# One product of keys and queries for both directions of a gated scan

## What is computed

```python
def _gla_scan(q, k, log_f, v, s0):
    mask = tril(ones(64, 64))
    def step(S, inp):                                   # chunks of 64 tokens
        qc, kc, gc, vc = inp
        b = cumsum(gc, axis=2)
        decay = exp(where(mask, b[:, :, :, None] - b[:, :, None], -inf))
        scores = einsum("bhtk,bhsk,bhtsk->bhts", qc, kc, decay)
        o = einsum("bhts,bhsv->bhtv", scores, vc) + einsum("bhtk,bhkv->bhtv", qc * exp(b), S)
        S = exp(b_end)[..., None] * S + einsum("bhsk,bhsv->bhkv", kc * exp(b_end - b), vc)
        return S, o

o_f, s_f = _gla_scan(qh, kf, gf, vh, s0_f)
o_b, s_b = _gla_scan(flip(qh), flip(kb), flip(gb), flip(vh), s0_b)
o = o_f + flip(o_b)
```

## Time and profile before

| | |
|---|---|
| median of 3 runs | 3245.99 us (3244.85 to 3246.26) |
| the profiled execution | 3246.3 us |
| its span, first to last instruction | 3244.5 us |
| TensorE busy | 2983.4 us, 92% |
| VectorE, ScalarE, GpSimd busy | 854.6, 561.9, 99.8 us |
| mean granted TensorE clock | 0.955 |
| slabs of L969, chain's share | 38% |
| scores (L1054), busy | 95.1 us in 768 instructions |

### The profile page before, as it was taken

How to read it: one execution, slowest core, us unless ns; L and a number is a source line. 1 busy time by engine, 2 the same in 40 slices (tenths; PEclk the granted TensorE clock), 3 DMA queues, 4 the chain that set the end, 5 groups by cost and what they waited for, 6 DMA issues and landing times.

```text
span 3244.5 us, 37753 instructions
## 1 busy us (share of the span) xinstructions
PE 2983.4 (92%) x16694; PEld 2469.0 (76%) x16694; DVE 854.6 (26%) x1777; ACT 561.9 (17%) x814; POOL 99.8 (3%) x204
## 2 busy tenths in 40 slices
PE   6999999999999999999999999799989998676665
PEld 4878889988888788878888888688878887343332
DVE  1201045531554210010014553410046313111111
ACT  1100232113221110010033115210012331100000
POOL 0000001100110000000001010000000000000000
PEclk8999999999999999999999999899989999788888
DMA  8566433344333566654443334244433235699997
GB/s 317 222 255 252 149 137 128 117 145 153 130 120 126 200 223 240 224 221 153 151 151 135 121 134 144 81 152 155 149 114 127 104 104 233 291 431 429 430 430 334
DMA packets 74311, 641.79 MB, mean 198 GB/s; under 512 B 8096, under 2 KB 13344, under 8 KB 22432
## 3 DMA queue, kind: packets, MB, share of 16 engines
q1 hardware_dynamic: 68720, 631.27, 51.7%
q10 hardware_dynamic: 5424, 8.05, 0.7%
HBM read 638.24 MB, written 1.05 MB: 197 GB/s over the span
## 4 chain that ended last, share of the span: by engine, by line
PE 82%; DMA 12%; DVE 3%; ACT 2%; issue 1%; ACTq 0%; POOL 0%; DVEq 0%
PE ps L969 38%; PE ps L992 17%; DMA work<-in_w_moe 10%; PE ps L1154 6%; PE ps L1054 3%; PE ps L1003 3%; PE ps L980 2%; PE ps L1180 2%; PE ps L949 2%; PE ps L846 2%; PE ps L865 1%; DVE work L1578 1%; DMA ones<-in_ones 1%; DMA ring<-in_w_moe 1%; PE ps L1161 1%
## 5 line engine op out<-in xcount | busy, mean ns | idle before, releaser
L969 PE MATMUL ps<-h,ring 128*128 128x256 f32 x6016 | 1323.4, 381 | 6.2 <-ACT h L1338 6.2
L969 PEld LDWEIGHTS ps<-h,ring 128*128 128x128 f32 x6016 | 1140.1, 191 | 173.7 <-issue 18.9
L992 PE MATMUL ps<-work,ring 128*128 128x256 f32 x2464 | 542.4, 380 | 0.0
L992 PEld LDWEIGHTS ps<-work,ring 128*128 128x128 f32 x2464 | 464.5, 190 | 69.0 <-issue 6.6
L1578 DVE TENSOR_TENSOR work<-work,ps 128x512 f32<-128x512 f32 (+1 forms) x153 | 87.9, 574 | 773.0 <-PE ps L969 713.6
L1154 PE MATMUL ps<-h,ring 128*128 128x256 f32 x928 | 207.9, 383 | 6.6 <-DVE h L1584 6.6
L1154 PEld LDWEIGHTS ps<-h,ring 128*128 128x128 f32 x928 | 176.9, 192 | 34.9 <-issue 11.5
L1578 DVE TENSOR_TENSOR work<-work 128x128 f32<-128x128 f32 (+4 forms) x632 | 195.7, 367 | 29.5 <-ACT work L1357 13.9
L846 PE MATMUL ps<-work 128*32 128x256 f32 x1536 | 120.5, 483 | 81.5 <-DMA work<-in_w_moe 75.7
L846 PEld LDWEIGHTS ps<-work 128*32 128x32 f32 x1536 | 67.2, 138 | 133.4 <-issue 121.3
L1305 ACT ACTIVATE work<-ps 128x512 f32<-128x512 f32 x77 | 46.0, 597 | 649.5 <-PE ps L969 649.3
(11 more groups left out here) (250 smaller groups left out, 1899.4 us busy)
## 6 DMA issues: line engine op xcount, KB each, us to landing
ring<-in_w SPq DMA_DIRECT2D x182, 1024.0 KB, 4.8
work<-in_w_moe SPq DMA_DIRECT2D x32, 4096.0 KB, 23.4
ring<-in_w_in SPq DMA_DIRECT2D x80, 1024.0 KB, 4.7
ring<-in_w_ada SPq DMA_DIRECT2D x72, 1024.0 KB, 6.1
ring<-in_w_moe SPq DMA_DIRECT2D x16, 4096.0 KB, 24.5
ring<-in_w SPq DMA_DIRECT2D x56, 896.0 KB, 4.6
ring<-in_w_out SPq DMA_DIRECT2D x16, 1024.0 KB, 4.8
ring<-in_w_mem SPq DMA_DIRECT2D x4, 1024.0 KB, 4.8
```

The costliest lines, as they stand in the source:

```text
L969: last = nc.tensor.matmul(ps[:, b, c * L:c * L + L], w[:, k * L + c * P:k * L + c * P + P], h[:, k, cols], start=(k == 0), stop=(k == KD - 1))
L992: last = nc.tensor.matmul(ps[:, b, c * L:c * L + L], w[:, k * L + c * P:k * L + c * P + P], hid[:, k0 + k, :], start=(k0 + k == 0 and c == 0),
```

## The change

The array `ex[:, 0, lev]` of a level now holds keys of both directions, and `ex[:, 1, lev]` queries of both: at each level the forward direction's key blocks are the backward direction's query blocks, so each array is full. One product then gives both directions' scores of a tile; its mask keeps both off-diagonal quarters. The eighth product uses `ksum`, the sum of both directions' keys, formed once a pass into the half of `glamask` that is free now. Score and value stages go by head and tile. The plan gives a head six bundles, one of them empty; the decays of a head follow the last products of the head before. In the first pass (28 gaps) there are 27 bundles and not 28, in the second (30) 27 and not 28, in the third (30) 25 and not 26. The semaphores' counts are halved where stages are. The core of the diff:

```diff
 def heads(l, s):
-    for hd in range(8):
-        more = hd + 1 < 8
-        out.append([("score", l, s, hd, 0)] + ([("decay", l, s, hd + 1)] if more else []))
-        out.append([("score", l, s, hd, 1), ("value", l, s, hd, 0)] + ([("times", l, s, hd + 1)] if more else []))
-        out.append([("value", l, s, hd, 1)] + ([("inter", l, s, hd)] if l == 0 else [])
-                   + ([("head", l, s, hd // 2)] if hd % 2 else []))
+    out = [[("decay", l, s, 1)], [("times", l, s, 0)]]
+    for hh in range(4):
+        out += [[], [("score", l, s, hh, 0)], [("score", l, s, hh, 1), ("value", l, s, hh, 0)]]
+        last = [("value", l, s, hh, 1)] + ([("inter", l, s, hh)] if l == 0 else []) + [("head", l, s, hh)]
+        if hh + 1 < 4:
+            out += [last + [("decay", l, s, 2 * hh + 2)], [("decay", l, s, 2 * hh + 3)], [("times", l, s, hh + 1)]]
+        else:
+            out.append(last)
     return out
...
-    side = [[("gmlp", 0, 1), ("decay", 0, 1, 0)], [("times", 0, 1, 0)]] + heads(0, 1) + [[("osquare", 0, 1)], [("osum", 0, 1)]]
+    side = [[("gmlp", 0, 1), ("decay", 0, 1, 0)]] + heads(0, 1) + [[("osquare", 0, 1)], [("osum", 0, 1)]]
...
-        gm = shaped(glamask[:], 2, 8, P)
+        gm = shaped(glamask[:, 0:8 * P], 8, P)
+        ksum = shaped(glamask[:, 8 * P:16 * P], 4, L)
...
                         for lev in range(8):
-                            lo, hi = (ex[:, d, lev, tc],) * 2 if lev < 7 else (kk[:, d, hh, tc], qq[:, hh, tc])
+                            kl, ql = (ex[:, 0, lev, tc], ex[:, 1, lev, tc]) if lev < 7 else (ksum[:, hh, tc], qq[:, hh, tc])
...
-                    elif kind == "decay":
+                    elif kind == "decay" and stage[3] % 2:
                         l, s, hd = stage[1:]
-                        act.wait_ge(dec_in, 8 * PASS[l, s] + hd + 1)
-                        nc.scalar.activation(ex[:, hd % 2, :, :], ex[:, hd % 2, :, :], ACT.Exp)
-                        nc.scalar.activation(eb[:, s, hd, :], be[:, s, hd, :], ACT.Exp).then_inc(dec_out, 1)
+                        act.wait_ge(dec_in, 4 * PASS[l, s] + hd // 2 + 1)
+                        nc.scalar.activation(ex[:, 0, :, :], ex[:, 0, :, :], ACT.Exp).then_inc(dec_out, 1)
+                        nc.scalar.activation(ex[:, 1, :, :], ex[:, 1, :, :], ACT.Exp)
+                        nc.scalar.activation(eb[:, s, hd - 1:hd + 1, :], be[:, s, hd - 1:hd + 1, :], ACT.Exp).then_inc(dec_out, 1)
...
+                def both_keys(l, s):
+
+                    if PASS[l, s]:
+                        dve.wait_ge(sc_done, 8 * PASS[l, s])
+                    else:
+                        dve.wait_ge(const_in, 16 * N_CONST)
+                    own(tt(ksum, kk[:, 0], kk[:, 1], add))
...
                         l, s, hd = stage[1:]
-                        d = hd % 2
-                        if hd >= 2 and l == 0:
-                            dve.wait_ge(hd_done, 8 * PASS[l, s] + hd - 1)
-                        elif hd >= 2:
-                            dve.wait_ge(pv_done, 32 + 2 * (hd - 1))
+                        hh, d = divmod(hd, 2)
+                        p = PASS[l, s]
+                        if hh and d == 0:
+                            dve.wait_ge(sc_done, 8 * p + 2 * hh)
+                            if l == 0:
+                                dve.wait_ge(hd_done, 4 * p + hh)
                         early, late, ee, le = sums(hd, s)
                         for lev in range(6):
...
-                            dst_e, dst_l = early_late(blocks(ex[:, d, lev, :], m), d)
+                            keys, _ = early_late(blocks(ex[:, 0, lev, :], m), d)
+                            _, queries = early_late(blocks(ex[:, 1, lev, :], m), d)
...
-                        dve.wait_ge(dec_out, 8 * PASS[l, s] + hd + 1)
-                        for lev in range(7):
-                            m = 1 << lev
-                            _, late = early_late(blocks(ex[:, d, lev, :], m), d)
-                            _, ql = early_late(blocks(qq[:, hh, :], m), d)
-                            tt(late, late, ql, mul)
-                        tt(ex7[:, hd, :] if l else ex[:, d, 7, :], ex[:, d, 7, :], qq[:, hh, :], mul).then_inc(xq_done, 1)
+                        dve.wait_ge(dec_out, 8 * PASS[l, s] + 2 * hh + 2)
+                        q = qq[:, hh, :].unsqueeze(1)
+                        tt(ex[:, 1, 0:7, :], ex[:, 1, 0:7, :], q.to_broadcast([P, 7, L]), mul)
+                        tt(ex7[:, 2 * hh:2 * hh + 2, :] if l else ex[:, :, 7, :], ex[:, :, 7, :], q.to_broadcast([P, 2, L]), mul
+                           ).then_inc(xq_done, 1)
...
-                        own(tt(pm, psf[:, 2048:3072].rearrange("p (v t) -> p v t", v=8), gm[:, d, :, :], mul))
+                        own(tt(pm, psf[:, 2048:3072].rearrange("p (v t) -> p v t", v=8), gm, mul))
...
-                    pool.wait_ge(dec_out, 8 * PASS[l, s] + hd + 1)
+                    l, s, hh = stage[1:]
+                    pool.wait_ge(dec_out, 8 * PASS[l, s] + 2 * hh + 1)
                     for lev in range(7):
                         m = 1 << lev
-                        early, _ = early_late(blocks(ex[:, d, lev, :], m), d)
-                        ke, _ = early_late(blocks(kk[:, d, hh, :], m), d)
-                        nc.gpsimd.tensor_tensor(early, early, ke, ALU.mult)
-                    nc.gpsimd.tensor_tensor(ex[:, d, 8, :], ex[:, d, 8, :], kk[:, d, hh, :], ALU.mult).then_inc(xk_done, 1)
+                        for d in range(2):
+                            keys, _ = early_late(blocks(ex[:, 0, lev, :], m), d)
+                            k_in, _ = early_late(blocks(kk[:, d, hh, :], m), d)
+                            nc.gpsimd.tensor_tensor(keys, keys, k_in, ALU.mult)
+                    pool.wait_ge(dec_out, 8 * PASS[l, s] + 2 * hh + 2)
+                    nc.gpsimd.tensor_tensor(ex[:, :, 8, :], ex[:, :, 8, :], kk[:, :, hh, :], ALU.mult).then_inc(xk_done, 1)
```

## The result

The changed kernel takes 3192.4 us, the median of four runs (3190.96 to 3193.94), against 3246.12 us for the kernel before (four runs). The ratio is 0.9835 with a 95% interval of 0.9818 to 0.9852, so 53.7 us went. The profiled execution took 3192.05 us, its span 3190.1 us.

A forecast was written before the change was run, and what follows sets the result against it. TensorE, busy nearly throughout the scan stages, was taken as the bound: 3246.3 us minus 48.2 of removed work minus 5.05 at the first scores gives 3193.0 us, forecast 3193 us, range 3188 to 3203 us (0.87).

The forecast's parts named there:

- TensorE's removed work, 48.2 us: In the three passes 24 score and 24 value stages leave TensorE, 24 x (1.79 + 0.22) = 48.2 us.
- The first scores, 5.05 us: TensorE's waits at each pass's first score, 0.56, 0.56 and 2.08 us, plus 1.85 us of clock in the third, go.
- VectorE's and ScalarE's relief at nothing: VectorE loses 75.8 us of masks and sums, ScalarE has fewer table loads; off the chain, so worth 0.
- The sum of the keys at nothing: One added VectorE instruction of 1.225 us a pass; shifts the third pass's decays by some 0.5 us, costs no wait.
- The prediction's own sign: In the profile after, GpSimd ends over 2 us before the first score of a head.
- The preparation of a head, 19.9 to 22.6 us, 2.5 us or more to spare: Decays, exponential and GpSimd's products before a head's first score fit in four slabs, 25.1 to 27.6 us; 0 new waits.
- The shared port: VectorE's two long products and GpSimd's take turns on SBUF, adding 2.7 us to a head's preparation; the room covers it.
- The end of the first pass, 0.1 us of room, and the transfers: VectorE's norm ends 0.1 us before the output projection's first slab, and weight slabs keep up at 151 GB/s; both 0.
- the first's: Rival 1: half the first-score waits stay, or some heads wait a little; 3203 us, upper end of the 0.87 range.
- The second: Rival 2: preparation just misses at each of 12 heads, 47 us of waits and clock, 3240 us; in full 0.03.
- third: Rival 3: GpSimd's products take twice as long beside VectorE's, 81 us given back at 9 heads, 3274 us; 0.03.
- The fourth: Rival 4: slabs can't come faster, TensorE waits for weights where it scored; all 53 us stay, 3246 us; 0.01.

The follow-up runs named there:

- early-score kernel: The changed kernel with each head's first score one bundle earlier, in the place of the empty one, its second score where it was; 3227.7 us, ratio 0.9942.

## Why the prediction was right, point by point

- **TensorE's removed work, 48.2 us.** Right, by two experiments: 40.9 us for 43 from the kernel before (42.8 us of it inside the passes), 43.5 us for 43 from the changed one. The places above give 16.6 us for the first pass, where there is no clock in the sum.
- **The first scores, 5.05 us.** Right; in the second and third passes also with nothing else changed, where both waits went and 4.7 us for 4.5.
- **VectorE's and ScalarE's relief at nothing.** Right for VectorE: 92 us put back changed nothing. ScalarE's fewer table loads were not tried apart; TensorE waited for it nowhere in the passes.
- **The sum of the keys at nothing.** Right, but by 1.45 us only. In the third pass the first decay began 19.20 us behind the start of the slabs (1675.73 to 1694.93 us) and not 18.63 as before (1709.39 to 1728.02), so it came 0.57 us later for my 0.5. GpSimd ended at 1715.72 us, TensorE came at 1717.17: 1.45 us of room, between my 0 and 2.7. The prediction's own sign, GpSimd ending over 2 us before the first score of a head, failed there and at the first pass's fourth head, 2 of 12; no wait came of it.
- **The preparation of a head, 19.9 to 22.6 us, 2.5 us or more to spare.** The result was right and this bound was not. GpSimd's part came out at 9.5 us (8.29 + 1.26), within my 8.2 to 10.9. But at the first pass's fourth head the chain ran from 594.25 us, VectorE's first instruction of it, to 617.3 us, GpSimd's last: 23.1 us, and TensorE came at 619.02, 1.7 us of room and not 2.5. The step left out is the plan's own order: the second decay stands one bundle behind the first, with the evacuation of a down slab between, so VectorE stood still until TensorE had finished that slab:

```profile
600.28 0.88 DVE L1589 SCALAR_TENSOR_TENSOR x<-ps,mod,x 128x256 f32<-128x256 f32 x2 [1.52 <-issue]
601.08 0.68 DVE L1598 TENSOR_TENSOR_SCAN work<-keep,work 128x256 f32<-128x256 f32 x1
```

  I had counted work (0.69 us for an evacuation) where the queue also has a wait (1.5 us), so the two decays took 11.3 us and not 9.6. That the first score was still met rests on the 2.5 us of margin, not on a right chain.
- **The shared port.** The trace agrees with what the Trainium skill says (SBUF — State Buffer, Who interferes with whom), that whoever starts second is blocked for the other's full length: one GpSimd instruction of 2.264 us among ones of 0.457, beside a VectorE instruction of 2.13 us. Counted as in the prediction, with both of VectorE's products, the rule makes it 2.7 us more for the 14; they took 2.2 us more than apart, 1.8 us behind the long product and 0.4 us behind the short one.
- **The end of the first pass, 0.1 us of room, and the transfers.** Nothing moved: the projection slabs began without a bracket, and at 134 to 144 GB/s no slab was awaited.
- **The rivals.** None of the first's waits came. The second and third didn't happen, and the early first score showed how near the second was: at one slab less (two at one head) nine of twelve heads wait. The fourth is out by the windows.
- **The total.** 3193 us against 3192.4 us is closer than the terms were known: the runs of the changed kernel spread over 3 us. That part is luck; what the experiments bear out are the terms.

## What to carry to other kernels

Where one engine's timeline has no gaps, count its instructions on the path and believe the product; 92 us of work on an engine with cover were worth 0, and 40 to 50 us on the full engine were worth themselves. When a change gives up an overlap, add up the whole preparation in queue order, waits for neighbouring stages included, and compare it with the slabs between at the tightest place: here 1.5 to 1.7 us were left, and a distance one slab shorter cost 35 us. The first use in a stage is such a place, since what prepares it starts late there.

## What was unexpected of the hardware

The granted clock doesn't follow the length of an idle stretch alone. In the early-score kernel it stayed at 2.4 GHz behind 3.32 and behind 2.04 us of idle time and fell behind 3.42 and 3.25 us; in the kernel before it fell behind 2.08 us. Nor is it the same from one execution to the next: behind 2.33 us of idle time at the same place behind the passes the same 16 instructions took 3.69 us in the kernels before and after, and 5.38 us with half the products and with the sum of the keys three times. Where it fell, the price at the first scores hardly differed: 1.55 to 1.86 us at five places of the early-score kernel, 1.85 us in the kernel before and 1.9 us with half the products. Where it stayed up behind 2.04 and 3.32 us, the first transposes took 0.19 us more and nothing else did. Behind the passes it differed: behind 4.2 us of idle time the next slab took 9.25 us in the changed kernel and 8.09 us with the sum of the keys three times, where 7.07 is its time at full clock. So a stall of 2 to 4 us at a first score was worth its length and either 0.2 us or 1.5 to 1.9 us more, and a sum that rests on it carries both.
